# A two-block transformer on one Trainium2 core: the second block's layer loop written out, with a narrower last feed-forward and a shorter way to the output

## What is computed

```python
h = concatenate([meta, x])               # 16 meta tokens ahead of 512 tokens: 528
h = layer_norm(h, ln_in_g, ln_in_b)
for l in range(2):
    h = layer_norm(ALPHA * h + 0.5 * swiglu_ffn(h, ffn1_w13[l], ffn1_w2[l]), ln_g[l, 0], ln_b[l, 0])
    h = layer_norm(ALPHA * h + token_mix(h, ...), ln_g[l, 1], ln_b[l, 1])
    h = layer_norm(ALPHA * h + 0.5 * swiglu_ffn(h, ffn2_w13[l], ffn2_w2[l]), ln_g[l, 2], ln_b[l, 2])
return h[:, 16:]                         # the meta tokens are dropped

def swiglu_ffn(x, w13, w2):              # w13: 1024 x 2*2752, w2: 2752 x 1024
    a, u = split(x @ w13, 2)
    return (silu(a) * u) @ w2
```

## Time and profile before

| | |
|---|---|
| time, median of 3 runs | 3579.97 us (3576.8 to 3580.01) |
| time of the profiled execution | 3576.85 us |
| its span | 3575.1 us |
| busy: PE, weight loads | 3377.7 us, 2785.4 us |
| busy: DVE, ACT, POOL | 1039.9, 829.7, 984.4 us |
| mean granted TensorE clock | 0.973 |
| first block | 0 to 1401 us |
| first layer of the second block | 1417 to 2480 us |
| second layer | 2487 to 3562 us |
| its last feed-forward | 3146 to 3543 us |
| transposes, copies and output | 3564.8 to 3575.1 us |

### The profile page before, as it was taken

One profiled execution on the slowest core, in us unless ns is written; L12 is line 12 of the kernel. 1 busy time (PEld: TensorE's weight loads), 2 busy tenths in 40 slices (PEclk: granted clock), 3 DMA queues, 4 the chain that ended last, 5 costly groups with the idle time before them and its releaser, 6 DMA issues. The chain is left out here.

```text
span 3575.1 us, 54497 instructions
## 1 busy us (share of the span) xinstructions
PE 3377.7 (94%) x23664; PEld 2785.4 (78%) x23664; DVE 1039.9 (29%) x1640; ACT 829.7 (23%) x1067; POOL 984.4 (28%) x415
## 2 busy tenths in 40 slices
PE   7989989978799998999999999999999999999997
PEld 2456579974444444999989789998999999789996
DVE  3034655552321214111145321113111155321113
ACT  2043311101000003322242142214222242142223
POOL 0021043410000001343345034343434345033433
PEclk9999999988899999999999999999999999999998
DMA  9241100002799996222121022222122121022221
GB/s 374 97 147 45 48 1 1 1 1 95 304 428 428 429 429 262 77 95 95 66 95 72 24 88 81 92 83 95 71 95 95 66 95 72 24 95 95 76 80 42
DMA packets 37157, 443.10 MB, mean 124 GB/s; under 512 B 5697, under 2 KB 6593, under 8 KB 10945
## 3 DMA queue, kind: packets, MB, share of 16 engines
q1 hardware_dynamic: 34400, 434.20, 31.0%
q10 hardware_dynamic: 2530, 5.57, 0.4%
HBM read 437.65 MB, written 2.10 MB: 123 GB/s over the span
## 5 line engine op out<-in xcount | busy, mean ns | idle before, releaser
L1942 POOL TENSOR_TENSOR w_lo<-low,w_hi 128x2048 fp32r<-128x2048 f32 (+2 forms) x162 | 709.7, 4381 | 1862.5 <-ACT w_hi L1937 1862.0
L1952 PE MATMUL PS<-h_hi,w_hi 128*128 128x264 f32 x3136 | 639.7, 285 | 1.2 <-POOL w_lo L1942 1.1
L1952 PE MATMUL PS<-h_lo,w_hi 128*128 128x264 f32 x3136 | 640.6, 286 | 0.0
L1952 PE MATMUL PS<-h_hi,w_lo 128*128 128x264 f32 x3136 | 639.7, 285 | 0.0
L1952 PEld LDWEIGHTS PS<-h_hi,w_hi 128*128 128x128 f32 x3136 | 488.1, 188 | 2.4 <-issue 2.2
L1952 PEld LDWEIGHTS PS<-h_lo,w_hi 128*128 128x128 f32 x3136 | 486.7, 188 | 0.0
L1952 PEld LDWEIGHTS PS<-h_hi,w_lo 128*128 128x128 f32 x3136 | 486.0, 189 | 0.0
L1937 ACT ACTIVATE w_hi<-low 128x2048 fp32r<-128x2048 f32 (+2 forms) x162 | 295.2, 1822 | 465.2 <-PE PS L1952 456.0
L1952 PE MATMUL PS<-g_hi,w_hi 128*128 128x264 f32 (+1 forms) x1408 | 295.7, 291 | 3.3 <-ACT low L2030 3.3
L2051 DVE TENSOR_TENSOR low<-low,PS 128x528 f32<-128x528 f32 x84 | 59.2, 704 | 805.7 <-PE PS L1952 768.3
L1952 PE MATMUL PS<-g_lo,w_hi 128*128 128x264 f32 (+1 forms) x1408 | 287.2, 285 | 0.0
(11 more groups left out here) (347 smaller groups left out, 4319.6 us busy)
## 6 DMA issues: line engine op xcount, KB each, us to landing
arena<-wts_dram SPq DMA_DIRECT2D x117, 2048.0 KB, 18.1
low<-wts_dram SPq DMA_DIRECT2D x70, 2048.0 KB, 7.7
low<-wts_dram SPq DMA_DIRECT2D x12, 1536.0 KB, 6.6
arena<-na_bias_dram SPq DMA_DIRECT2D x16, 768.0 KB, 4.1
arena<-x_dram ACTq DMA_DIRECT2D x1, 2048.0 KB, 29.7
arena<-x_dram SPq DMA_DIRECT2D x1, 2048.0 KB, 7.8
low<-wts_dram SPq DMA_DIRECT2D x2, 1024.0 KB, 5.1
out_dram<-high SPq DMA_DIRECT2D x4, 512.0 KB, 2.6
```

What stands on the lines that cost most here:

```text
L1942: nc.gpsimd.tensor_tensor(lo, raw, hi.bitcast(F32), ALU.subtract).then_inc(w_l.sem, 1)
L1952: mm = nc.tensor.matmul(bank(b, h), w[wi], halves(x[xi])[:, h, :], start=(first and i == 0), stop=(last and i == 2))
```

## The change

Five things are changed.

1. The layer loop is written out: PE, ACT, POOL and DVE have the code of both layers one behind the other, with constants in place of register values. PE's list grows from 5328 to 8989 rows as the compiled program lists them.
2. In the last feed-forward (layer 1, `w == 1`; `final`, `fin`) the 16 meta tokens are left out. Each sum then has 512 columns and fits in one bank, so a product is 3 matmuls of 512 columns in place of 6 of 264. ACT and DVE read and write 512 columns there too.
3. The last layer norm makes neither `h_hi` nor `h_lo`; ACT makes only `hT`. The splits of the two pieces of a next layer go, and so does the dummy chunk.
4. The block `store` is gone. PE transposes feature tile k of `hT` for the four token tiles as soon as ACT has made it: tiles 0 to 3 into banks 0 to 3, then, once DVE has read the last of the spread deviations (banks 4 and 5), tiles 4 to 7 into banks 4 to 7. ACT copies banks 0 to 3 out between its own layer norm instructions, and at the end ACT and DVE copy two of the banks 4 to 7 each.
5. The output goes out in 8 DMAs of 256 KB, the first four halves of rows while the norm still runs.

The diff, cut to its core (the lines in which `halves(x)` only becomes `toks(x, fin)` and `bank(b)` becomes `sums(b, fin)` in silu, multiply, split and evacuation are left out):

```diff
+    def final(l, w):
+        return l == NL - 1 and w == 1
+
+    def toks(ap, fin):
+        return ap[:, NMETA:] if fin else halves(ap)
+
+    def sums(b, fin):
+        return PS[:, b, :] if fin else bank(b)
...
     def ln_dve(dve, l, uu, evacuate):
...
-            if 1 <= k <= LOV:
+            if 1 <= k <= LOV and not (l == NL - 1 and uu == 2):
                 low(k - 1)
...
     def ln_act(act, l, uu, gain, shift, next_split, second_split):
...
             ln_n.wait(act, l, uu, k + 1)
+            if l == NL - 1 and uu == 2:
+                nc.scalar.activation(hT[:, k, :], res[:, k, :], ACT.Identity, scale=gain[:, k:k + 1], bias=shift[:, k:k + 1]).then_inc(ln_f.sem, 1)
+                if k >= DK - TT:
+                    out_rows(act, k - (DK - TT))
+                continue
...
     def ln_pool(pool, l, uu):
+        if l == NL - 1 and uu == 2:
+            return
...
     def split_act(act, l, i):
+        if l == NL - 1 and i >= NS:
+            return
...
-    def product(b, w, x, first, last):
+    def product(b, w, x, first, last, fin=False):
 
         for i, (wi, xi) in enumerate([(0, 0), (0, 1), (1, 0)]):
+            if fin:
+                mm = nc.tensor.matmul(PS[:, b, :], w[wi], x[xi][:, NMETA:], start=(first and i == 0), stop=(last and i == 2))
+                continue
             for h in range(2):
                 mm = nc.tensor.matmul(bank(b, h), w[wi], halves(x[xi])[:, h, :], start=(first and i == 0), stop=(last and i == 2))
...
+    fo_ps, fo_a, fo_v, stored = sem("fo_ps"), sem("fo_a"), sem("fo_v"), sem("stored")
+    ot = Map(high, g_at, E["TOTAL"], HIGH).take(TT, D)
+
+    def turned(t, k, b):
+        s = NMETA + t * P
+        return nc.tensor.transpose(PS[:, b + t, k % 4 * P:(k % 4 + 1) * P], hT[:, k, s:s + P], C["ident"])
+
+    def out_rows(act, t):
+        act.wait_ge(fo_ps, t + 1)
+        nc.scalar.activation(ot[:, t, 0:512], PS[:, t, :], ACT.Copy).then_inc(fo_a, 1)
...
-            for n in range(RAW, NL * LAYC + 1):
+            for n in range(RAW, NL * LAYC):
...
+            for half, done in enumerate((fo_a, fo_v)):
+                for t in range(TT):
+                    if half and t % 2 == 0:
+                        sp.wait_ge(fo_a, TT + t // 2 + 1)
+                    else:
+                        sp.wait_ge(done, (t // 2 if half else t) + 1)
+                    sp.dma_start(E["out"][t * P:(t + 1) * P, half * 512:(half + 1) * 512], ot[:, t, half * 512:(half + 1) * 512]).then_inc(stored, 16)
+            sp.wait_ge(stored, 32 * TT)
...
         def _(pe):
...
-            with pe.Fori(0, NL) as l:
+            for l in range(NL):
...
+            for k in range(4):
+                ln_f.wait(pe, NL - 1, 2, k + 1)
+                for t in range(TT):
+                    last = turned(t, k, 0)
+                    if k == 3:
+                        last.then_inc(fo_ps, 1)
+            ln_n.wait(pe, NL - 1, 2, DK)
+            for k in range(4, DK):
+                ln_f.wait(pe, NL - 1, 2, k + 1)
+                for t in range(TT):
+                    last = turned(t, k, 4)
+                    if k == DK - 1:
+                        last.then_inc(fo_ps, 1)
```

More of the change, by code:

```diff
@@ L1953, in product, with first_two, each @@
         return mm
-    def first_two(pe, l, uu, wts):
-        ends = []
+    def first_two(pe, l, uu, wts, fin=False):
+        def each(z, wi, x, first, last):
+            if fin:
+                return nc.tensor.matmul(PS[:, 2 * z, :], wts[z][wi][:, k, :], x[:, NMETA:], start=first, stop=last)
+            for h in range(2):
+                mm = nc.tensor.matmul(bank(2 * z, h), wts[z][wi][:, k, :], halves(x)[:, h, :], start=first, stop=last)
+            return mm
         for k in range(DK):
@@ L1961, in first_two @@
                 for wi in range(2):
-                    for h in range(2):
-                        nc.tensor.matmul(bank(2 * z, h), wts[z][wi][:, k, :], halves(h_hi[:, k, :])[:, h, :], start=(k == 0 and wi == 0), stop=False)
+                    each(z, wi, h_hi[:, k, :], k == 0 and wi == 0, False)
             lo_ready(pe, l, uu, k)
[L1965 to L1969, removed]
+            ends = [each(z, 0, h_lo[:, k, :], False, k == DK - 1) for z in range(2)]
+        return ends
     UP = 2 * FT - 1
@@ L1983, in ffn_pe @@
                 if f == 0:
-                    for last in first_two(pe, l, 2 * w - 1, [[x[:, z] for x in wt] for z in range(2)]):
+                    for last in first_two(pe, l, 2 * w - 1, [[x[:, z] for x in wt] for z in range(2)], fin):
                         last.then_inc(up_ps.sem, 1)
@@ L1991, in ffn_pe @@
                     for k in range(DK):
-                        last = product(4 * (f % 2) + 2 * z, [x[:, z, k, :] for x in wt], (h_hi[:, k, :], h_lo[:, k, :]), k == 0, k == DK - 1)
+                        last = product(4 * (f % 2) + 2 * z, [x[:, z, k, :] for x in wt], (h_hi[:, k, :], h_lo[:, k, :]), k == 0, k == DK - 1, fin)
                     last.then_inc(up_ps.sem, 1)
@@ L2006, in ffn_pe @@
                     r = slice(0, 64 if f0 + f == FT - 1 else P)
-                    last = product(2 * (m % apart), [x[r, m % 2, f, :] for x in wt], (g_hi[r, f, :], g_lo[r, f, :]), f == 0, f == nf - 1)
+                    last = product(2 * (m % apart), [x[r, m % 2, f, :] for x in wt], (g_hi[r, f, :], g_lo[r, f, :]), f == 0, f == nf - 1, fin)
                     if g == len(GROUPS) - 1 and f in (1, nf - 2):
@@ L2039, in ffn_pool @@
     def ffn_pool(pool, l, w):
-        for i in range(w * S_FFN2 + 2, w * S_FFN2 + S_MIX + 2):
+        for i in range(w * S_FFN2 + 2, min(w * S_FFN2 + S_MIX + 2, NS if final(l, w) else NS + 2)):
             split_pool(pool, l, i)
     def ffn_dve(dve, l, w):
+        fin = final(l, w)
         for g, (f0, nf) in enumerate(GROUPS):
@@ L2060, in evacuate @@
                 dn_ps.wait(dve, l, w * DN + g * DK + m + 1)
-                nc.vector.scalar_tensor_tensor(halves(res[:, m, :]), bank(2 * (m % apart)), 0.5, halves(res[:, m, :]),
+                nc.vector.scalar_tensor_tensor(toks(res[:, m, :], fin), sums(2 * (m % apart), fin), 0.5, toks(res[:, m, :], fin),
                                                ALU.mult, ALU.add).then_inc(dn_sb.sem, 1)
@@ L2550, in _ @@
                         ffn_act(act, l, 1)
+            for t in (0, 2):
+                act.wait_ge(fo_ps, TT + t + 1)
+                nc.scalar.activation(ot[:, t, 512:], PS[:, 4 + t, :], ACT.Copy).then_inc(fo_a, 1)
         @block.gpsimd
@@ L2556, in _ @@
             ln_pool(pool, None, 0)
-            with pool.Fori(0, NL) as l:
+            for l in range(NL):
                 ffn_pool(pool, l, 0)
@@ L2567, in _ @@
             ln_dve(dve, None, 0, None)
-            with dve.Fori(0, NL) as l:
+            for l in range(NL):
                 ffn_dve(dve, l, 0)
```

55 lines of the change are left out of this document (15 added, 40 removed).

## The result

The changed kernel takes 3549.82 us, the median of 4 runs (3546.26 to 3552.22), against 3579.49 us for the kernel before, run beside it (3576.8 to 3580.01). The ratio is 0.9918, with a 95% interval of 0.9901 to 0.9935. So 29.7 us are gone, where 52.6 were forecast: the direction was right, the size was not, and the time lies outside the range. The profiled execution took 3549.33 us, its span is 3547.5 us.

A forecast was written before the change was run, and what follows sets the result against it. The prediction took PE's own pace as the bound and summed 42.5 (feed-forward) + 0.4 (loop) + 9.7 (tail) = 52.6 us saved, giving 3526 us, range 3519 to 3533, or 3518 to 3542 with the constant overhead.

The forecast's parts named there:

- PE is the bound: Whole kernel: PE, busy for 94% of the span, sets the pace and must remain the bound after the change.
- the wait at f = 2: Third inner tile of the last feed-forward: PE's wait for POOL's piece grows from 0.43 us to about 2.
- the 1.6 us for it: Range allowance: idling at f = 2 may send PE's clock to 1.2 GHz for a few microseconds, costing about 1.6 us.
- The narrower feed-forward: Last feed-forward from f = 2: 1464 pairs fall from 0.2448 to 0.2158 us each, saving 42.5 us.
- The price goes by columns: Rival for the last feed-forward: 0.2374 us per 512-column matmul, saving 10.8 us there, 3558 in all; chance 0.03.
- the constant overhead: Rival: 12.4 ns stay with every fp32r matmul, 0.2257 us each, saving 28 us there, 3540 in all; chance 0.11.
- the high end: Upper bound for one 512-column matmul: 0.262 us, by the slope between fp32r rows of 256 and 264 columns.
- Slower: Rival: long fp32r rows cost more than their columns, 0.262 us, adding 25 us in the feed-forward, 3593; chance 0.04.
- much faster: Rival: matmuls of 512 columns overlap at 0.131 us each, 167 us would go, 3400; chance 0.01.
- The written-out loop: Passage between layers: PE's 5.82 us issue gap goes, but POOL's piece for f = 2 catches it; 0.4 us saved.
- I count nothing: Elsewhere in the written-out loop: register waits becoming waits on constants are already hidden and save nothing.
- The tail: Last norm and output: dropping rounded parts and overlapping transposes and copies with the norm saves 9.7 us.

The follow-up runs named there:

- e1_bench: Changed kernel plus a block of matmuls by PE alone behind the output, in several formats, lengths and weight widths; fp32r with 512 columns took 0.2317 us each.
- e5_256: Changed kernel with the last feed-forward's 512 tokens as two halves of 256 in two banks; 3553.81 us, ratio 0.9924.
- e3_unroll: Kernel before with only the layer loop written out, narrow last feed-forward and old end kept; 3575.02 us, ratio 0.9991.
- e8_bench2: Changed kernel plus a second block of matmuls alone: zero operands, fewer partitions, other lengths, bf16 spacing; fp32r with 512 columns and zero tokens took 0.2317 us.
- e2_narrow: Changed kernel with its last feed-forward back at 528 tokens in two halves of 264; 3566.19 us, ratio 0.9968.

## Why the prediction was right or wrong

- **PE is the bound** and stays it: right. POOL's pieces come in time but for the two waits named, 1.9 us; the clock stays at 1.00 behind the wait at f = 2 (from 3174 to 3180 us), so the 1.6 us for it were not needed.
- **The narrower feed-forward, 42.5 us: wrong.** The step that failed reads: "the 11 to 12 ns of the fp32r rows are the next weight load not quite hidden behind 107 to 110 ns of streaming, and that behind 213 ns it is hidden, as in the fp32 rows", with 0.2158 us as its value. The runs put 0.2317 in its place, over the 0.225 from which the prediction called itself wrong, and with pairs of 0.2447 it is 1464 x 0.0130 = 19.0 us; 19.1 were measured. The count of pairs and the choice to count nothing before f = 2 were right. The surcharge is no piece of a weight load: a weight tile a quarter as wide leaves it nearly whole (e1_bench), and merging two matmuls into one removes 2.2 ns of it (e5_256). It grows with the fp32r columns, from 11 ns at 256 to 18 at 512. I carried the pace of fp32 over to fp32r because the weight tile was the same; the streamed format was not.
- **The rivals.** "The price goes by columns" (0.2374, 3558) and the constant overhead (0.2257, 3540) enclose what was measured; 0.2317 is 5.7 ns from the first and 6.0 from the second. I gave 0.03 to the first, and my argument against it was the same fp32 row. The two fp32r paces of the kernel before, 0.1179 for 256 columns and 0.1224 for 264, held the hint: from one to the other the surcharge grows. I had that slope and used it only as the high end, where at 0.262 it is 30 ns too much: 8 columns are too short a distance to take a slope from. "Slower" was refuted with the forecast: 0.2317 is under the 0.2517 from which it decides. So was "much faster".
- **The written-out loop, 0.4 us:** right for the passage, too small for the rest. The gap of 5.8 us went and POOL's wait took its place: 0.6 us from mark to f = 2 in e3_unroll and in the changed kernel. But "I count nothing" for the waits on constants elsewhere does not hold. From the mark ahead of a mixer to the last one in it, the kernel before takes 258.1 us in both layers; the twelve profiles with the loop written out have 256.7 to 257.9 us in their 24 mixers. The second feed-forward of the first layer takes 403.1 us, at the same dense pace, where it took 403.5. The profiles before and after, which both keep the dense pace of 11.75 us up to the last feed-forward, differ by 2.7 us up to there, and that is the better value for this term. There is only one profile of the kernel before, and what in the written-out loop saves the time, the constants in the waits or something else, stays open.
- **The tail, 9.7 us: right**, and nearly step by step: 11.1 us to the last `hT` (forecast 11.2), 14.3 to the last copy (14.4), and 9.2 to 9.7 us in all. The last 16 transposes ran at a granted clock of 0.50, the half microsecond that the prediction allowed for. ACT's copies did hold up the last `hT`, by about half a microsecond, as the sum had it, but PE's transposes of the tiles before were still running then, and DVE's part of the norm went on undisturbed.
- **The sum.** 19.1 + 2.7 + 9.7 = 31.5 us; measured 29.7, 34.2 and 31.8, on average 31.9. With the 0.6 us of the passage alone for the loop it would be 29.4. The medians of the changed kernel lie 4.8 us apart, so they do not decide between the two.

## What to carry to other kernels

In these runs a matmul's price per column hangs on the operand format: here 512 columns cost 0.2159 us in bf16 and 0.2317 in fp32r. Take the pace from rows of the same format at two lengths that lie well apart, and let the line through them decide for a third length before a row of another format does: through 256 and 384 columns it gives 0.233 for 512, through 256 and 264 of the kernel before 0.262. Fewer, longer matmuls brought little here (2.2 ns a pair); fewer columns brought most of the gain. A gap on the bounding engine is worth only what the next wait behind it leaves over: 5.8 us of issue were worth 0.6.

## What the runs showed that I had not expected

- **fp32r has a surcharge by the column at the full clock, and none at the low one.** In the product for f = 0 of the last feed-forward, which runs beside the layer norm ahead of it at a granted clock of 0.50 (1.2 GHz), the same matmuls stand 0.427 us apart (the two rows below are three steps, 1.28 us), which is 512 columns at 1.2 GHz:

```profile
3150.50:3153.00 2.50, 2.50 (x7) 1.96 (x6) 2.36 (x5) 1.91 (x3) 0.00 (x0) 0.50 0.69 242
```

```profile
3150.98 0.63 PE L1980 MATMUL PS<-h_hi,w_hi 128*128 128x512 f32 x1
...
3152.26 0.63 PE L1980 MATMUL PS<-h_hi,w_lo 128*128 128x512 f32 x1
```

  In e8_bench2 it is the same over a long stretch: 0.427 us for 512 columns and 0.267 for 320 while the clock is 0.50. Together with the four-byte spacing this looks like a limit in reading the streamed operand. That is a reading, and the mechanism stays open.
- **A dense stream on 32 partitions lost the clock.** In e8_bench2 PE went from 64 partitions at a granted clock of 1.00 to 32, without a gap and with all other engines idle. The first 16 or so matmuls on 32 partitions still stand 0.232 us apart; from 3661.7 us on it is 0.427, the lower level, and so it stays to the end of that row and into the next, on 128 partitions, where the clock is full again from 3699.3 us on. Over the stretch shown the mean is 0.55:

```profile
3640.00:3656.00 16.00, 16.00 (x71) 12.73 (x70) 0.00 (x0) 0.00 (x0) 0.00 (x0) 1.00 0.00 1
3658.00:3694.00 36.00, 36.00 (x92) 27.57 (x93) 0.00 (x0) 0.00 (x0) 0.00 (x0) 0.55 0.00 0
```

- **The dense pace of 264 columns has two values**, 11.68 and 11.75 us for an inner tile, which change from run to run and from one feed-forward to another in one run: 0.07 x 2928 / 96 = 2.1 us over the feed-forward. e2_narrow ran at the lower one throughout, which is why it puts the narrower feed-forward at 17 us and the first pair of profiles at 19. With 512 columns every profile shows 11.12. The four feed-forwards in the one profile of the kernel before all ran at 11.75; whether the lower pace comes there too is not known. The cause stays open.
